# The tail of a transformer block on one core: earlier squares and joins, a later sum, and the last gate unit in two tiles

## The reference, cut to what matters

```python
def conv_ffn(x, w_up, conv_w, conv_b, w_down):
    ...
    return (jax.nn.silu(g) * up) @ w_down

for i in range(DEPTH):
    ...
    h = h + rms_norm(mix, post_mix_g[i])
    f = conv_ffn(rms_norm(h, pre_ffn_g[i]), w_up[i], conv_w[i], conv_b[i], w_down[i])
    h = h + rms_norm(f, post_ffn_g[i])
    gate = jax.nn.sigmoid(rms_norm(h, ple_norm_g[i]) @ w_ple_gate[i])
    h = h + gate * (p[i] @ w_ple_proj[i])
```

## Time and profile before

| | |
|---|---|
| runs (3) | 2526.78, 2528.34, 2530.46 us |
| median | 2528.34 us |
| the profiled execution's own time | 2526.62 us |
| its span (first to last instruction) | 2524.8 us |
| PE busy | 2298.5 us, 91% |
| DVE, ACT, POOL busy | 58%, 43%, 10% |
| mean granted TensorE clock | 0.955 |
| chain that ended last, by engine | PE 16%, DVE 3%, ACT 1% |

### The profile page before, as it was taken

One profiled execution on the slowest core, in us unless ns is written; L12 is line 12 of the kernel. 1 busy time (PEld: TensorE's weight loads), 2 busy tenths in 40 slices (PEclk: granted clock), 3 DMA queues, 4 the chain that ended last, 5 costly groups with the idle time before them and its releaser, 6 DMA issues. The chain is left out here.

```text
span 2524.8 us, 35857 instructions
## 1 busy us (share of the span) xinstructions
PE 2298.5 (91%) x15154; PEld 1879.3 (74%) x15154; DVE 1464.4 (58%) x2198; ACT 1081.1 (43%) x1709; POOL 260.1 (10%) x146
## 2 busy tenths in 40 slices
PE   5999889789999967998889999997998889999996
PEld 3988667678888855776588888866876688888865
DVE  2133573649778763456677666355466676666353
ACT  3121472557667553245534333243235534333242
POOL 0000101523223210101010000011101010000011
PEclk7999999899999979999989999999999989999998
DMA  8111006212111102230112222312230012222311
GB/s 347 60 51 67 34 1 229 89 50 60 51 51 51 52 26 106 102 115 18 46 67 85 99 100 100 106 53 100 101 117 1 18 67 100 90 94 100 109 66 69
DMA packets 35200, 205.18 MB, mean 81 GB/s; under 512 B 3936, under 2 KB 5472, under 8 KB 14816
## 3 DMA queue, kind: packets, MB, share of 16 engines
q1 hardware_dynamic: 35040, 202.88, 22.8%
HBM read 200.77 MB, written 2.10 MB: 80 GB/s over the span
## 5 line engine op out<-in xcount | busy, mean ns | idle before, releaser
L278 PE MATMUL ps<-a_high,w_high 128*128 128x512 f32 (+1 forms) x1680 | 632.4, 376 | 35.6 <-DVE a_low L2390 22.7
L279 PE MATMUL ps<-a_low,w_high 128*128 128x512 f32 (+1 forms) x1680 | 621.5, 370 | 0.0
L280 PE MATMUL ps<-a_high,w_low 128*128 128x512 f32 (+1 forms) x1680 | 620.9, 370 | 0.0
L278 PEld LDWEIGHTS ps<-a_high,w_high 128*128 128x128 f32 x1680 | 320.6, 191 | 100.5 <-DVE w_low L2004 19.6
L2004 DVE TENSOR_TENSOR w_low<-raw_ring,w_high 128x2048 fp32r<-128x2048 f32 x102 | 234.0, 2294 | 269.7 <-ACT w_high L1998 265.0
L279 PEld LDWEIGHTS ps<-a_low,w_high 128*128 128x128 f32 x1680 | 321.2, 191 | 54.1 <-issue 2.5
L280 PEld LDWEIGHTS ps<-a_high,w_low 128*128 128x128 f32 x1680 | 321.0, 191 | 52.3
L1998 ACT ACTIVATE w_high<-raw_ring 128x2048 fp32r<-128x2048 f32 x102 | 195.3, 1914 | 365.3 <-PE ps L280 279.4
L278 PE MATMUL ps<-x_high,place_high 128*128 128x512 f32 (+1 forms) x720 | 261.3, 363 | 13.0 <-POOL place_low L270 7.9
L279 PE MATMUL ps<-x_low,place_high 128*128 128x512 f32 (+1 forms) x720 | 255.7, 355 | 0.0
L280 PE MATMUL ps<-x_high,place_low 128*128 128x512 f32 (+1 forms) x720 | 255.5, 355 | 0.0
(11 more groups left out here) (372 smaller groups left out, 4002.3 us busy)
## 6 DMA issues: line engine op xcount, KB each, us to landing
raw_ring<-w_dram SPq DMA_DIRECT2D x112, 1024.0 KB, 4.9
arena<-w_dram SPq DMA_DIRECT2D x24, 1024.0 KB, 8.3
place_raw<-wc_dram SPq DMA_DIRECT2D x48, 512.0 KB, 3.6
place_raw<-w_dram SPq DMA_DIRECT2D x11, 1024.0 KB, 4.9
ab_raw<-w_dram SPq DMA_DIRECT2D x10, 1024.0 KB, 5.0
x<-xT_dram SPq DMA_DIRECT2D x4, 512.0 KB, 14.2
out_dram<-x SPq DMA_DIRECT2D x1, 2048.0 KB, 7.2
arena<-r_dram SPq DMA_DIRECT2D x2, 992.0 KB, 7.3
```

Source lines behind the costliest of these rows:

```text
L278: nc.tensor.matmul(out, wh, xh, start=start, stop=False)
L279: nc.tensor.matmul(out, wh, xl, start=False, stop=False)
L280: return nc.tensor.matmul(out, wl, xh, start=False, stop=stop)
```

## The change

Five things change, the same in both layers.

1. DVE's join of dn11B moves from k = 7 to k = 4 in `half("dn", 0)`, and its square on ACT from behind the eight operands to behind the fourth.
2. PE's "dn1" sum moves from behind p3 to behind p5. p4 and p5 write banks that dn10B and dn11B used, so they now wait for the joins.
3. ACT's squares of X for the first half of the tokens move from behind the weight split to ahead of the "dn1" root. Those of the second half move ahead of the weight split. 
4. SP's fetch of the second gate unit waits for PE's p7 in place of ACT's last `keep`.
5. The last gate unit g3 is handed on tile by tile: DVE, ACT and DVE treat it as two parts of 512 columns in place of one of 1024.

```diff
-                        sp.wait_ge(S.kept, KT)
+                        sp.wait_ge(S.pe_tile, job_no["p7"])
...
                         for j in range(KT):
+                            if j in (4, 5):
+                                pe.wait_ge(S.joined, j + 5)
                             if j >= 6:
                                 pe.wait_ge(S.kept, j - 5)
...
-                            if j == 3:
+                            if j == 5:
                                 pe.wait_ge(S.res_root, sum_no["dn0"])
                                 sums("dn1", halves[1], sq)
...
                         for k in range(2, KT):
                             operand("dn", 0, k)
-                        joined(10, 3, 1)
+                            if k == 3:
+                                joined(10, 3, 1)
...
+                        next_squares(0)
                         root("dn1", 0, halves[1])
                         for k in range(KT):
                             if k + 4 < KT:
                                 keep(k + 4)
                             operand("dn", 1, k)
+                        next_squares(1)
                         split(u_g + 1, "dn11B")
-                        next_squares(0)
-                        next_squares(1)
                         root("ple", 1, slice(0, L))
...
-                        for m in range(4):
-                            finished(f"g{m}")
+                        for i, (m, ks) in enumerate(gate_parts):
+                            finished(jobs[job_no["g0"] - 1 + i])
```

More of the change, by code:

```diff
@@ L2736, in stage_tail @@
                 jobs += [f"up{j}" for j in range(2, FT)] + [f"dn{i}" for i in range(10)]
-                jobs += ["dn10A", "dn11A", "dn10B", "dn11B"] + [f"p{j}" for j in range(KT)] + [f"g{m}" for m in range(4)]
+                jobs += ["dn10A", "dn11A", "dn10B", "dn11B"] + [f"p{j}" for j in range(KT)] + [f"g{m}" for m in range(3)] + ["g3a", "g3b"]
                 job_no = {name: i + 1 for i, name in enumerate(jobs)}
@@ L2751, in stage_tail @@
                 SPLIT_UP, SPLIT_DN, SPLIT_G = 0, 2 * KT, 2 * KT + FT
+                gate_parts = [(m, slice(2 * m, 2 * m + 2)) for m in range(3)] + [(3, slice(6, 7)), (3, slice(7, 8))]
                 def tile2(b):
@@ L2952, in _ @@
                                             ready=SPLIT_G + KT if m + h == 0 else None)
-                            last.then_inc(S.pe_tile, 1)
+                                if m == 3 or h == 1:
+                                    last.then_inc(S.pe_tile, 1)
                             if m == 0:
@@ L3182, in half @@
                                         meet("wo2B", 2, 1)
[L3183 to L3187, removed]
+                                if k == 4 and name == "dn" and weights:
+                                    join(3, 1)
+                                if k == 7 and name == "wo" and weights:
+                                    meet("wo3B", 3, 1)
                         def chunk(v):
@@ L3260, in _ @@
                         split_low(dve, u_g + 1)
-                        for m in range(4):
-                            finished(f"g{m}")
+                        for i, (m, ks) in enumerate(gate_parts):
+                            finished(jobs[job_no["g0"] - 1 + i])
                             if m == 0:
                                 inverse("ple", 1, slice(0, L))
-                            pg = fbuf[:, 2 * m:2 * m + 2, :]
-                            nc.vector.tensor_tensor(pg, tile2(PAIR[m]),
-                                                    rstd[:, 1, :].unsqueeze(1).to_broadcast([P, 2, L]), O.mult)\
+                            pg, n = fbuf[:, ks, :], ks.stop - ks.start
+                            b = PAIR[m] + ks.start - 2 * m
+                            nc.vector.tensor_tensor(pg, PS[:, b:b + n, :],
+                                                    rstd[:, 1, :].unsqueeze(1).to_broadcast([P, n, L]), O.mult)\
                                 .then_inc(S.dve_out, 1)
@@ L3270, in _ @@
                                 split_low(dve, u_g + m + 2)
[L3271 to L3273 removed]
+                            dve.wait_ge(S.sigmoid, i + 1)
+                            link(nc.vector.tensor_tensor(pg, pg, pp[:, ks, :], O.mult))
+                            nc.vector.tensor_tensor(X[:, ks, 0:L], X[:, ks, 0:L], pg, O.add)
             stage_front()
```

5 lines of the change are left out of this document (2 added, 3 removed).

## The result

| | before | changed |
|---|---|---|
| runs | 4: 2526.78 to 2530.46 us | 4: 2504.34 to 2509.28 us |
| median | 2528.81 us | 2506.39 us |
| ratio | | 0.9913, 95% interval 0.9895 to 0.9930 |
| profiled execution, its span | 2526.62, 2524.8 us | 2504.34, 2502.6 us |
| PE busy | 2298.5 us | 2292.8 us |

The row of the kernel before has one run more than the prediction had, 2529.28 us. The forecast was 2504 us with a range of 2499 to 2513. Its working can be checked piece by piece if both traces are laid on a common mark. I use the start of the join of dn11A on DVE, 2423.57 in the second layer before and 2412.41 now, so a time of now is compared with one of before after 11.16 is added. From that mark to the end of the layer's last addition to X I call **the stretch**. It holds all that the change touches.

What follows compares the result with a forecast made beforehand. PE, busy 91% of the span, was held to gain only from its idle stretches around the tail stage. Gains of 7.5 + 2.4 + 2.1 = 12.0 us a layer, 24 for two, gave 2504 us, range 2499 to 2513.

Steps and rivals of the forecast that it cites:

- "ple" sum earlier: PE's sum behind g0 starts at 2467.8 in place of 2475.28, 7.5 us gained a layer.
- The join and the two tiles: Join of dn11B and dn1 sum moved: sum ready 3 us before ACT needs it, alone worth nothing to PE.
- The first squares: Four squares ahead of the dn1 root: root 0.4 later, 0.8 lost on DVE's scalings, last high operand 1.3 earlier.
- The second squares and POOL: Squares start at 2460.45; POOL's last three adds end at 2465.85, or 2468.0 if DVE's split comes before the third.
- The fetch: Second gate unit's fetch lands by 2453.7, ACT wants it at 2462.6; worth nothing by itself.
- g0 and its clock: First gate unit on PE ends at 2467.3 at full clock, 2468.0 with a half-clock start; 2467.8 taken.
- The clock behind: Without a wait before the "ple" sum, it and g1 run at full clock: 34.4 for 36.84, 2.4 us gained.
- The last unit: Last gate unit in two parts: 2.7 us from PE's last result to X in place of 4.83, 2.1 gained.
- (a): Rival: clock stays full over the layer boundary, up to 2.2 us more gained there; 2500 to 2502, chance 0.15.
- (b): Rival: clock at half through all of g0, only 2.8 us a layer gained, 2522.7; chance in full 0.06.
- (c): Rival: low clock held on through g1, X 6 us later than before, 2540 in all; chance 0.04.
- (d): Rival: POOL and DVE delay each other around 2461 to 2468, or the split for g1 does; 2524, chance 0.04 with no change.

Runs made afterwards that it cites:

- E2: The changed kernel with the join of dn11B, the sum dn1 and the fetch put back as before; stretches 81.82 and 83.08 us, median 2509.61 us, ratio 0.9931.
- E1: The kernel before with only the last gate unit in two parts; stretches 91.47 and 91.34 us, median 2525.07 us, ratio 0.9989.
- E5: The changed kernel with all eight squares put back behind the weight split; stretches 87.13 and 87.07 us, median 2514.74 us, ratio 0.9935.
- E3: The changed kernel with ACT taking the dn1 root before the first half's four squares; stretches 81.92 and 81.94 us, median 2502.54 us, ratio 0.9896.
- E4: The changed kernel with DVE's low split of the second gate unit waiting for POOL's last add; stretches 81.63 and 81.65 us, median 2509.36 us, ratio 0.9925.
- E10: The changed kernel with the squares behind the weight split and the fetch's old wait; stretches 87.29 and 87.38 us, 2514.3 us in one run.
- E6: The changed kernel with five unused matmuls behind p7, ahead of g0; stretches 82.31 and 82.30 us, median 2507.30 us, ratio 0.9905.
- E7: The changed kernel with three unused matmuls in PE's pause at the layer boundary; 655.00 us between the stretches, median 2499.92 us, ratio 0.9879.
- E8: The changed kernel with the first four squares issued between operands 4 to 7, root before copies; stretches 79.35 and 79.34 us, median 2503.32 us, ratio 0.9887.

## Why the prediction was right, point by point

| term, us a layer | predicted | measured (layer 2) |
|---|---|---|
| "ple" sum earlier | 7.5 | 6.92 |
| from that sum's start to the last result | 2.4 | 36.84 - 34.69 = 2.15 |
| from the last result to X | 2.1 | 4.83 - 2.80 = 2.03 |
| sum | 12.0 | 11.10 |

*The join and the two tiles.* Right in that g0 does not wait for them, and that the sum has its result ready before ACT wants it. "Worth nothing" holds beside the early squares (E2), not by itself (E1 to E5). One step was wrong: "the wait in front of them (all eight operands of half 0) is unchanged, since DVE does the same work in another order". It is the same work, but POOL's add for the moved join now falls on a DVE scaling (1.48 in place of 0.48). That makes ACT's last operand 1.00 later against the mark (21.09 in place of 20.09). The moved square no longer stands between it and the copies, which gives back half: ACT's copies start 0.49 later, and the root 0.8 later than before and not 0.4. So one of the prediction's own signs, a root within 0.5 us of its old place, was not met, though the sum was in time as it said.

*The first squares.* The 0.8 taken for the two scalings was right: 1.61 - 0.88 = 0.73. E3 shows that it is the edge of a hole: two us earlier and 2.43 would be lost. Only because the squares delay the root does DVE arrive when POOL is nearly through.

The Trainium skill's page "GPSIMD Engine Reference" (Specifications), by which GpSimd contends with VectorE instructions that have two SBUF inputs, is borne out by these rows, and by E4's, where an add of two SBUF inputs on GpSimd is the one that waits. The note on 2-port modes in the Trainium skill's page "Advanced Engine Details and Errata" (VectorE Performance Modes) is not the whole of it: if only those instructions were held up, E3 would have gained the full 2.08.

*The second squares and POOL.* The squares start at 2449.69 + 11.16 = 2460.85, predicted 2460.45. POOL's end was given by the two ends 2465.85 and 2468.0; it was 2468.31, 0.3 beyond the later one. Both causes are known: the 0.4 of the step above, and the third add behind the split, 3.36 and not 1.3 (E4 removes that). This is the term that was mis-sized, the 7.5 that came out at 6.9.

*The fetch.* ACT's weight split starts at 2451.78, directly behind the squares, so it does not wait for the transfer, as predicted. Where the squares are late, the earlier fetch is worth 0.16 and 0.31 (E10).

*g0 and its clock.* g0 ended at 2467.96, predicted 2467.8, with the clock at half at its start, as I had let it be. That the two agree so well is partly luck. The prediction had 2467.3 for a full clock, put 0.7 on the low one and took 2467.8 in between; E6 has the full clock and ends g0 at 44.44 behind the mark, 2468.01. So the end at the full clock was set 0.7 too early, and the low clock cost nothing.

*The clock behind.* The sum took 1.98, predicted 1.76 and under 2.2.

*The last unit.* 2.80 against 2.7, and E1 confirms it alone.

*The rivals.* (a), the boundary, did not come: a pause shorter by 2 us, still 4.77, left the clock at half. E7 shows that the prize was there: 2.2 in the mean at the boundary itself, as I had put on it, and 2.8 against this trace. The eleven matmuls of the prediction were those in its window, which ends at 1769.30 with the clock still at half; twelve were slow in the kernel before, fourteen in the changed one. (b) and (c), a low clock through g0 or g1, did not come; the clock was back 4.5 us behind the restart. (d) was right in its mechanism and wrong in its size: POOL and DVE do hold each other up around 2461 to 2468, for 2.1 us, of which 0.65 reach the end (E4).

The median is 2.4 above the forecast. The terms were 0.9 a layer too large, 1.8 for two; the remaining 0.6 lies within the scatter outside the stretches.

## What to carry to other kernels

Work that another engine will need is best issued in the gaps between the waits of the engine that issues it (E8), not in a block ahead of something urgent or behind something late; and two edits that shorten the same path are measured together and apart, since their gains do not add (E1, E2, E5). Before moving a GpSimd add, look at what VectorE does in those microseconds: three adds cost nothing while it runs a reciprocal, and 2.43 us beside scalings and an addition (E3). Where a pause of TensorE is followed by work that it bounds, a few unused matmuls in the pause can pay (E7); where the work behind is fed slowly, they do not (E6).

## What the runs showed of the hardware

- POOL and DVE exclude each other by whole instructions here, when both have two SBUF inputs: a 0.48 us scaling behind the start of an add takes 1.48, a 1.3 us add behind the start of a 2.29 us split takes 3.36. DVE's reciprocal with one input is not disturbed (1.75 with POOL idle, 1.75 and 1.74 with POOL busy), and neither are the adds (4.07 for three of them beside it, 4.16 with DVE out of the way in E4).
- After a pause the clock came back at different times in the same program: 2.8 us behind the restart in one layer of E2 and 5.9 in the other, 4.5 in the changed kernel. Behind the layer boundary 7 to 14 matmuls were slow, over the traces without E7's edit. An estimate should hold both ends.
- A clock at half costs nothing where the feed is about as slow as TensorE at half (g0 ends 44.44 behind the mark at the full clock in E6, 44.39 behind it in the changed kernel). At the layer boundary it cost what the slow matmuls took beyond their time at the full clock, 0.2 us each: 2.8 for fourteen of them (E7), 1.4 for seven (E4, whose first reciprocal lies at 27.85 against 26.46).
